# Sums of squares of a streaming encoder layer: two fp32r products of a high and a low part instead of one product in full precision

## What is computed

```python
h = rmsnorm(x)
qa, ka, va, qb, kb, vb, rb, a1, ga, gb = split(h @ w_in)
qa = rmsnorm(qa per head of 64, g_q); ka = rmsnorm(ka per head of 64, g_k)
oa = sliding_window_attention(qa, ka, va)           # 16 heads, 4 key heads
ob = rmsnorm(gated_linear_attention(qb, kb, vb, a1), g_ob) * silu(rb)   # 4 heads of 256
x = x + (sigmoid(ga) * oa + sigmoid(gb) * ob) @ w_out
x = x + (silu(h2 @ w_gate) * (h2 @ w_up)) @ w_down   # h2 = rmsnorm(x)
```

## Time and profile before

| | |
|---|---|
| median of 3 runs | 897.75 us |
| the profiled execution: its time | 897.51 us |
| its span | 895.5 us |
| PE busy | 875.3 us, 98% |
| VectorE (DVE) busy | 578.9 us, 65% |
| ScalarE (ACT) busy | 413.8 us, 46% |
| chain that ended last, by engine | PE 82%, DVE 11%, ACT 3%, DMA 2%, issue 2% |

### The profile page before, as it was taken

One profiled execution on the slowest core, in us unless ns is written; L12 is line 12 of the kernel. 1 busy time (PEld: TensorE's weight loads), 2 busy tenths in 40 slices (PEclk: granted clock), 3 DMA queues, 4 the chain that ended last, 5 costly groups with the idle time before them and its releaser, 6 DMA issues.

```text
span 895.5 us, 17243 instructions
## 1 busy us (share of the span) xinstructions
PE 875.3 (98%) x7061; PEld 847.7 (95%) x7061; DVE 578.9 (65%) x1156; ACT 413.8 (46%) x757; POOL 197.8 (22%) x131
## 2 busy tenths in 40 slices
PE   8989999999999999999999989999999999999998
PEld 6989999989998999999999979999999999999997
DVE  7773666676885446555455799973379853699622
ACT  7632543535555454545444575542155541365421
POOL 2200000000002323232334213235122153222350
PEclk9999999999999999999999999999999999999999
DMA  8531222221423121212117359853288723887322
GB/s 278 152 94 48 76 67 71 59 83 41 126 71 95 50 70 51 70 51 69 48 41 224 88 126 194 177 148 96 70 189 180 166 86 101 172 178 163 94 80 63
DMA packets 151028, 96.38 MB, mean 108 GB/s; under 512 B 5008, under 2 KB 140646, under 8 KB 150822
## 3 DMA queue, kind: packets, MB, share of 16 engines
q1 hardware_dynamic: 136326, 74.96, 29.2%
q0 software_dynamic: 9504, 17.31, 12.4%
q10 hardware_dynamic: 5120, 3.02, 1.2%
HBM read 71.45 MB, written 5.83 MB: 86 GB/s over the span
## 4 chain that ended last, share of the span: by engine, by line
PE 82%; DVE 11%; ACT 3%; DMA 2%; issue 2%; SPq 0%; POOL 0%; DVEq 0%; POOLq 0%
PE G L653 16%; PE G L655 15%; PE G L654 15%; PE X L932 4%; PE X L934 4%; PE X L935 4%; PE G L932 4%; PE G L934 3%; PE G L935 3%; PE X L863 2%; PE X L847 2%; PE X L832 2%; PE X L785 1%; PE X L773 1%; DVE w_lo L1785 1%
## 5 line engine op out<-in xcount | busy, mean ns | idle before, releaser
L653 PE MATMUL G<-h_hi,w_hi 128*128 128x272 f32 x1280 | 381.6, 298 | 3.4 <-DVE vB L1677 1.9
L655 PE MATMUL G<-h_hi,w_lo 128*128 128x272 f32 x1280 | 370.9, 290 | 0.0
L654 PE MATMUL G<-h_lo,w_hi 128*128 128x272 f32 x1280 | 369.2, 288 | 0.0
L653 PEld LDWEIGHTS G<-h_hi,w_hi 128*128 128x128 f32 x1280 | 241.7, 189 | 10.9 <-issue 7.0
L654 PEld LDWEIGHTS G<-h_lo,w_hi 128*128 128x128 f32 x1280 | 241.9, 189 | 0.8
L593 POOL TENSOR_TENSOR w_lo<-wraw,w_hi 128x1024 fp32r<-128x1024 f32 x54 | 139.0, 2581 | 468.2 <-DVE w_lo L1785 247.2
L655 PEld LDWEIGHTS G<-h_hi,w_lo 128*128 128x128 f32 x1280 | 241.4, 189 | 0.0
L1065 ACT ACTIVATE w_hi<-wraw 128x1024 fp32r<-128x1024 f32 (+1 forms) x129 | 134.5, 1045 | 60.2 <-PE G L655 35.2
L1265 ACT ACTIVATE prob<-prob,nm 128x256 f32<-128x256 f32 (+2 forms) x80 | 36.7, 460 | 64.3 <-DVE sd L1718 64.3
L2053 DVE TENSOR_TENSOR rs<-G,rv 128x544 f32<-128x544 f32 x23 | 16.7, 724 | 75.6 <-PE G L655 75.6
L1392 ACT ACTIVATE sq<-sq 128x544 f32<-128x544 f32 x22 | 14.5, 659 | 99.0 <-DVE sq L1940 99.0
(11 more groups left out here) (322 smaller groups left out, 1816.4 us busy)
## 6 DMA issues: line engine op xcount, KB each, us to landing
wraw<-in_w_in_dram SPq DMA_DIRECT2D x52, 512.0 KB
wraw<-in_w_gate_dram SPq DMA_DIRECT2D x22, 512.0 KB
wraw<-in_w_up_dram SPq DMA_DIRECT2D x22, 512.0 KB
csum<-csum POOLq DMA_DIRECT2D x44, 256.0 KB, 5.2
wraw<-in_w_down_dram SPq DMA_DIRECT2D x16, 448.0 KB
wraw<-csum POOLq DMA_DIRECT2D x22, 256.0 KB, 3.4
wraw<-in_w_out_dram SPq DMA_DIRECT2D x8, 512.0 KB
wraw<-in_w_down_dram SPq DMA_DIRECT2D x8, 512.0 KB
```

Source lines behind the costliest of these rows:

```text
L653: pe.matmul(o, w_hi[:, slot, kc, :], b_hi[:, kc, cols], start=(kc == 0), stop=False)
L654: pe.matmul(o, w_hi[:, slot, kc, :], b_lo[:, kc, cols], start=False, stop=False)
L655: mm = pe.matmul(o, w_lo[:, slot, kc, :], b_hi[:, kc, cols], start=False, stop=(kc == last))
```

## The change

The squares in sq are split like the weights: sq_hi is a copy into fp32r, sq_lo = sq - sq_hi. The sum of squares is then two fp32r products per half, head_ones x sq_hi and head_ones x sq_lo, added in PSUM; head_ones and the new all_ones are fp32r. For q and k tiles ACT makes sq_hi in read_out and DVE makes sq_lo (`square_low_part`); for GLA heads DVE makes both in gla_add. There is one buffer each for sq_hi and sq_lo. On PE the sums of q and k tiles go from step 3 to step 5 of the next tile, that of the last GLA head from step 6 to step 7. To make room, wa2 and lab share space with Ssmp and Sfin, and rbu with sq_lo.

```diff
--- before.py
+++ after.py
@@ -122,6 +122,12 @@
 
 
 POST_TILES = [n for n in range(N_IN) if USES[n] == 2]
+NORM_TILES = [n for n in POST_TILES if IN_TILES[n][0] in ("kA", "qA")]
+
+
+def norm_tiles_before(n):
+
+    return sum(m < n for m in NORM_TILES)
 
 
 def gemms(n):
...
@@ -224,19 +230,23 @@
         vc = tensor(mix, "vc", [P, KV_A * HD])
         raw = tensor(mix, "raw", [P, 2, T])
         kout = tensor(mix, "kout", [P, 2, 2 * P])
-        head_ones = tensor(mix, "head_ones", [P, P])
+        head_ones = tensor(mix, "head_ones", [P, P], F32R)
+        all_ones = tensor(mix, "all_ones", [P, P], F32R)
+        sq_hi = tensor(mix, "sq_hi", [P, T], F32R)
+        squares = ExitStack()
+        sq_lo = tensor(squares, "sq_lo", [P, T], F32R)
+        squares.close()
+        rbu = tensor(mix, "rbu", [P, T])
         dist = tensor(mix, "dist", [P, 2 * P])
 
 
         gla = ExitStack()
         Sin = tensor(gla, "Sin", [P, HEADS_B, DV])
-        wa2 = tensor(gla, "wa2", [P, HEADS_B * DK])
         prow = tensor(gla, "prow", [24, P])
         srow = tensor(gla, "srow", [1, HEADS_A])
         kc_tok = tensor(gla, "kc_tok", [P, KV_A * HD])
         cmask = tensor(gla, "cmask", [P, P])
         reset = tensor(gla, "reset", [P, NJ, P + 1])
-        lab = tensor(gla, "lab", [P, NJ, P + 1])
         a1T = tensor(gla, "a1T", [P, T])
         CB = tensor(gla, "CB", [P, HEADS_B, NJ, P + 1])
         dec = tensor(gla, "dec", [P, 2, NJ])
...
@@ -253,6 +263,10 @@
         tB = tensor(gla, "tB", [P, NJ * P])
         tC = tensor(gla, "tC", [P, NJ * P])
         vB = tensor(gla, "vB", [P, 2, NJ, DV])
+        gates = ExitStack()
+        wa2 = tensor(gates, "wa2", [P, HEADS_B * DK])
+        lab = tensor(gates, "lab", [P, NJ, P + 1])
+        gates.close()
         Ssmp = tensor(gla, "Ssmp", [P, 2, DV])
         Sfin = tensor(gla, "Sfin", [P, 2, DV])
         gla.close()
...
@@ -265,7 +279,6 @@
         prob = tensor(att_mem, "prob", [P, NB, GH, 2 * P])
         probT = tensor(att_mem, "probT", [P, 2, 2, 2, P])
         th = tensor(att_mem, "th", [P, 2, T])
-        rbu = tensor(att_mem, "rbu", [P, T])
         mx = tensor(att_mem, "mx", [P, NB, GH])
         nm = tensor(att_mem, "nm", [P, NB, GH])
         sd = tensor(att_mem, "sd", [P, NB, GH])
...
@@ -733,9 +748,11 @@
                     for j, (t0, nt) in enumerate(TOK):
                         mm = pe.transpose(ps[0:nt, j * P:(j + 1) * P], raw[:, n % 2, t0:t0 + nt], ident[:, :])
                 else:
+                    pe.wait_ge(sq_lo_ok, norm_tiles_before(n) + 1)
                     for b in range(2):
-                        mm = pe.matmul(ps[:, 512 * b:512 * b + TH], head_ones[:, :],
-                                       sq[:, n % 2, b * TH:(b + 1) * TH], start=True, stop=True)
+                        o, cols = ps[:, 512 * b:512 * b + TH], slice(b * TH, (b + 1) * TH)
+                        pe.matmul(o, head_ones[:, :], sq_hi[:, cols], start=True, stop=False)
+                        mm = pe.matmul(o, head_ones[:, :], sq_lo[:, cols], start=False, stop=True)
                 mm.then_inc(post_done, 1)
 
             def gla_scores(h):
...
@@ -793,8 +810,9 @@
             def gla_squares(h):
                 pe.wait_ge(gla_sum, h + 1)
                 for b in range(2):
-                    mm = pe.matmul(X[0][:, 512 * b:512 * b + TH], ones[:, :],
-                                   sq[:, 0, b * TH:(b + 1) * TH], start=True, stop=True)
+                    o, cols = X[0][:, 512 * b:512 * b + TH], slice(b * TH, (b + 1) * TH)
+                    pe.matmul(o, all_ones[:, :], sq_hi[:, cols], start=True, stop=False)
+                    mm = pe.matmul(o, all_ones[:, :], sq_lo[:, cols], start=False, stop=True)
                 mm.then_inc(gla_ssq, 1)
 
             def keys_out():
...
@@ -875,13 +893,13 @@
             for h in range(HEADS_B):
                 put(gate_tile(h), 2 + 4 * (h % 2), gate_logits, h)
             for n in POST_TILES:
-                put(n + 1, 3, second_use, n)
+                put(n + 1, 5 if n in NORM_TILES else 3, second_use, n)
             for h in range(HEADS_B):
                 late = h == HEADS_B - 1
                 put(gla_tile(h, 0), 7 if late else 3, gla_scores, h)
                 put(gla_tile(h, 1), 4 if late else 1, gla_updates, h)
                 put(gla_tile(h, 2) + late, 1 if late else 7, gla_outputs, h)
-                put(gla_tile(h, 3), 6, gla_squares, h)
+                put(gla_tile(h, 3), 7 if late else 6, gla_squares, h)
             put(KEYS_OUT, 7, keys_out)
             for u in range(NU + LAG):
                 n = UNIT0 + u
...
@@ -1231,6 +1249,9 @@
                     link(act.activation(h2(sq[:, s, :]), ps, ACT.Square))
                     g = G_K if kind == "kA" else G_Q
                     act.activation(h2(raw[:, s, :]), ps, ACT.Copy, scale=param[:, g:g + 1]).then_inc(set_free[s], 1)
+                    if norm_tiles_before(n):
+                        act.wait_ge(post_done, POST_TILES.index(NORM_TILES[norm_tiles_before(n) - 1]) + 1)
+                    act.activation(sq_hi[:, :], sq[:, s, :], ACT.Copy).then_inc(sq_hi_ok, 1)
                 elif kind == "ga":
                     if i == 0:
                         act.wait_ge(gla_norm, HEADS_B)
...
@@ -1486,9 +1507,11 @@
 
             dve.memset(ones[:, :], 1.0).then_inc(const_dve, 1)
             dve.memset(rv[:, 0:NJ], 1.0).then_inc(const_dve, 1)
-            link(dve.memset(head_ones[:, :], 0.0))
-            dve.memset(head_ones[0:HD, 0:HD], 1.0)
-            dve.memset(head_ones[HD:P, HD:P], 1.0)
+            link(dve.memset(rs[:, 0:P], 0.0))
+            dve.memset(rs[0:HD, 0:HD], 1.0)
+            link(dve.memset(rs[HD:P, HD:P], 1.0))
+            dve.tensor_copy(head_ones[:, :], rs[:, 0:P])
+            dve.tensor_copy(all_ones[:, :], ones[:, :])
             link(dve.memset(one[:, :], 1.0))
             dve.memset(eps[:, :], EPS).then_inc(const_dve, 1)
             link(dve.memset(a1T[:, :], 0.0))
...
@@ -1651,7 +1674,19 @@
             def gla_add(h):
 
                 dve.wait_ge(gla_sq, h + 1)
-                dve.tensor_tensor(sq[:, 0, :], sq[:, 0, :], sq[:, 1, :], ALU.add).then_inc(gla_sum, 1)
+                link(dve.tensor_tensor(sq[:, 0, :], sq[:, 0, :], sq[:, 1, :], ALU.add))
+                before = [n for n in NORM_TILES if n + 1 <= gla_tile(h, 3)]
+                if before:
+                    dve.wait_ge(post_done, POST_TILES.index(before[-1]) + 1)
+                link(dve.tensor_copy(sq_hi[:, :], sq[:, 0, :]))
+                dve.tensor_tensor(sq_lo[:, :], sq[:, 0, :], sq_hi[:, :].bitcast(F32),
+                                  ALU.subtract).then_inc(gla_sum, 1)
+
+            def square_low_part(n):
+
+                dve.wait_ge(sq_hi_ok, norm_tiles_before(n) + 1)
+                dve.tensor_tensor(sq_lo[:, :], sq[:, n % 2, :], sq_hi[:, :].bitcast(F32),
+                                  ALU.subtract).then_inc(sq_lo_ok, 1)
 
             def gla_norms(h):
                 k = NORMS.index(("gla", h))
...
@@ -1796,6 +1831,8 @@
             for n in range(N_IN):
                 if n == gate_tile(HEADS_B - 1) + 1:
                     empty_rows()
+                if n - 1 in NORM_TILES:
+                    square_low_part(n - 1)
                 if RING <= n + 2 < HANDOVER:
                     weight_low_part(n + 2)
                 for h in range(HEADS_B - 1):
```

More of the change, by code:

```diff
@@ L384, in mixer_program @@
         gla_sum = sem("gla_sum")
+        sq_hi_ok = sem("sq_hi_ok")
+        sq_lo_ok = sem("sq_lo_ok")
         gla_ssq = sem("gla_ssq")
```

## The result

The changed kernel takes 909.1 us (median of 4 runs, 907.4 to 909.75), the kernel before in the same session 897.4. The ratio is 1.0118, 95% interval 1.0102 to 1.0135: slower by 1.2%. The profiled execution took 909.71 us (span 907.7), against 897.51 (span 895.5) before: 12.2 us more.

The account below looks back on a forecast made before the run. PE, 98% busy, was taken to bound the kernel, with DVE close behind and becoming the bound in the qA tiles. 897.5 us plus 5.75 of lateness gave 903.3; 3.0 for three clock falls gave 906.3, range 901.5 to 909.0.

Parts of the forecast that it names:

- rival 2: More clock falls, also from 0.4 us waits of each qA tile, or the copy at 0.72: 908.5 or more; chance 0.10.
- the waits of 0.4 us: PE's waits in each qA tile, on which the saving of these tiles is spent: 0.4 us each.
- What PE saves: A sum on PE falls from 0.92 to 0.50 us, saving 0.42, 14 times: 5.9 us if nothing waits.
- The copy on DVE: Copy to sq_hi in each GLA head, taken at 0.44 us; at 0.72 it adds 0.28 per head.
- Three GLA sums: GLA heads 0 to 2: PE waits 0.87 for the low part and saves 0.42, so +0.45 us per head.
- Tiles 17 and 18: The two kA sums: PE waits 1.6 and 3.4 us for DVE's low part; the updates start 3.6 us late.
- First qA sum: Tile 21: PE arrives at 216.22, the low part is ready at 218.56, a wait of 2.3 us.
- Ring: qA tiles: DVE's and ACT's round becomes the bound, 6.94 us a tile against PE's new 6.54; it was 6.96.
- First turn: First turn of attention: already waited 0.93 on DVE's chain from tile 28; PE waits about 2.8 us more in all.
- The 5.75 us of lateness: DVE, then PE from attention's first turn, is 5.75 us late, which stays to the end: 903.3 us without clock falls.
- The clock: Granted clock falls behind the waits of 3.4, 2.3 and 2.8 us, 1.0 us each: 3.0 us added.
- PE-bound (891.6): Rival: DVE's low parts are ready when PE comes, 14 sums give 5.9 us, time 891.6; chance 0.06.

Follow-up runs that it names:

- Experiment 2: Only the four GLA sums split, q and k sums as in the kernel before: 901.07 us, 1.0028 of the kernel before.
- experiment 1: The changed kernel with the GLA sums back to one full product, only the ten kA and qA sums split: 904.39 us, 1.0071 of the kernel before.
- experiment 5: The changed kernel plus unused products on PE ahead of its three longest waits (11, 8 and 9 calls): 903.83 us, 1.0062 of the kernel before.
- experiment 7: The changed kernel with GLA sums full, subtraction and low part of weights moved in DVE's queue, ACT's copy earlier, q/k sums behind step 4: 897.79 us, 0.9992.
- experiment 3: The changed kernel with GLA sums full and, for q and k, sq_lo and its product left out: 895.71 us, 0.9978 of the kernel before.
- experiment 4: The kernel before with kA and qA sums split, subtraction on POOL, sq_hi ahead of ACT's raw copy, sums at old places: 907.26 us, 1.0102.
- Experiment 9: As experiment 7, with the low part of the weights also moved behind unit_max in the first two attention units: 893.68 us, 0.9953 of the kernel before.
- experiment 11: As Experiment 9, but kA sums in full precision again, only the eight qA tiles split: 889.95 us, 0.9903 of the kernel before.
- experiment 10: The kernel before with both moves of the low part of the weights from Experiment 9, without the split: 895.32 us, 0.9970 of the kernel before.

## Why the prediction was right, and what it missed

Forecast 906.3, measured 909.1, just over the upper end of the range (909.0). The sign and the mechanism of the waits hold. The number lies where rival 2 put it (908.5 or more, with a chance of 0.10): a fall more did come, but not from the waits of 0.4 us named there, and the copy was the fast one. Of the 12.2 us between the profiled executions 8.8 were forecast; the other 3.4 are 0.64 of the start, 0.3 of the waits (6.04 before any fall, for 5.75), 1.2 of the three falls and 1.5 of a fourth, less 0.2 given back in the last third.

- **What PE saves.** A new sum takes 0.50 us (two halves of two products, 0.126 apart), but behind a wait its first product takes 0.23 instead of 0.126 (99.38 to 99.61), so a sum that is waited for saves about 0.1 less. That was not in the working, and it is 0.54 a head where 0.45 was forecast.
- **The copy on DVE.** I chose 0.44 between 0.44 and 0.72. It measured 0.444. The subtraction, 0.72, measured 0.718. ACT's copy was hidden, as assumed: DVE's round is what its own operations and the root make it.
- **Three GLA sums.** Forecast waits 0.87; the profile puts 0.70 on the wait, and the lateness of 0.54 each includes the 0.1 above. Experiment 2 isolates it.
- **Tiles 17 and 18.** Forecast 1.6 and 3.4, measured 1.51 and 3.13 (1.52 and 3.14 in experiment 1). Updates 3.6 late forecast, 6.06 measured; 0.64 of the rest is the start, 0.3 the heads, 1.5 the first fall.
- **First qA sum.** 2.3 forecast, 2.27 measured. **Ring.** 6.94 forecast, 6.93 measured, from tile 24 on; in the two tiles behind the second fall PE was the later one. The forecast waits of 0.4 are the gaps of 0.30 without a bracket and the slower first product. **First turn.** About 2.8 forecast, 2.53 measured.
- **The waits without the clock.** The 5.75 us of lateness can be checked at the first turn: 9.33, less the 0.64 of the start, 1.55 of the first fall and 1.1 of the second, leaves 6.04; experiment 5, without these falls, has 6.0.
- **The clock is the step that failed, in size.** I took "1.0 us for each since part of a fall can lie in the wait" for three falls. Three came, where they were placed, and cost 4.2 (experiment 5), not 3.0. The first and the third cost 1.55 each: the low clock begins at the product behind the wait or a little later, and it is PE's own queue, the critical one, that runs through it. The second cost 1.1 at the first turn, since DVE's ring sets that, and DVE lost only the 0.92 and 0.18 us in which it waited for PE. The estimate of 1.25 from the earlier trace rows was too low for two of them.
- **Three falls of three was in part luck.** The waits of 3.13 and 3.14 us at tile 18 were followed by a fall in both profiles. Of six waits between 2.2 and 2.8 us three were (2.27 and 2.53 in the changed kernel, 2.20 in experiment 7) and three were not (2.54, 2.72 and 2.37 at the first turn of experiments 1, 3 and 4), and the wait of 1.8 in the MLP was in 5 of 13 profiles. So the rule of the forecast, a fall for every wait longer than the one of 1.86, does not hold; the length of a wait alone does not decide in this range. What else does is open.
- **The fourth fall** was foreseen in rival 2 as a possibility and from other causes (the 0.4 us waits, which did nothing). It came behind a wait that was there before. The four executions of the changed kernel have mean clocks of 0.989 to 0.991, that is five falls or about that by the scale above, so it is no accident of the profiled one. It does not go by how late PE comes there: in experiment 2 PE was 2.7 us late and the fall came, in experiment 1 it was 5.6 late and it did not. Why is open.
- **The rivals.** PE-bound (891.6) needed DVE 3.4 us sooner at tile 18 and a ring under 6.54. Experiment 9 comes near that by another order on DVE and ACT (with the GLA sums back in full precision), and the sign turns; experiment 11 also leaves the kA sums as they were.

## What to carry to other kernels

Before work is moved from the busiest engine to another, look for the stage in which the other one's round is nearly as long as the bottleneck's: here DVE is 65% busy over the span, but in the eight qA tiles its shortest round (6.30 us, 6.94 with the subtraction) was already close to PE's tile (6.96, 6.54 with the new sum), and eight of the ten subtractions stand in those. If the split is wanted, put its extra operation where the helper waits for something else, and leave it out where the consumer is next in line (the kA tiles, the GLA heads): split at the eight qA tiles alone, with the subtraction, the low part of the weights and ACT's copy moved, the kernel went from 1.2% slower to 1.0% faster (four executions), though 0.3% of that is the moves of the weights alone (experiment 10). And count the clock with the waits: behind half of the waits of 2.2 to 2.8 us on TensorE here it fell, and such a fall cost up to 1.55 us more than the wait itself.

## What the runs showed of the hardware that I had not expected

- A subtraction on POOL (1.56 us) lengthened the DVE operation beside it from 0.72 to 1.75 to 1.78 us; an idle engine was not a free one.
- The same wait on PE (1.76 and 1.77 us) was followed by a fall of the granted clock in one profile and not in the other, and so were waits of 2.2 to 2.8 us: 2.20, 2.27 and 2.53 were followed by one, 2.37, 2.54 and 2.72 were not. A fall cost 1.55 us of a product stream at 0.227 us a product instead of 0.126.
- Work on PE made the kernel faster: 28 calls of products that nobody reads gained 5.0 us, by keeping the clock at 2.4 GHz through three waits.
